# Hybrid DeltaNet / attention step: weight ring with a running place, dense stages written out straight, four output chunks side by side behind each norm, down projection begun on early rounded activations

## The reference, cut to what matters

```
layer 0: h = modulate(rmsnorm(x));  [gated DeltaNet || differential attention](h @ w_in) @ w_out
         h = modulate(rmsnorm(x));  x += gate * ((silu(h @ w_g) * (h @ w_u)) @ w_down)      # D_FF = 2816
layer 1: h = modulate(rmsnorm(x));  multi-head latent attention (w_in, w_uq, w_ukv, w_out)
         h = modulate(rmsnorm(x));  top-2-of-8 expert SwiGLU (D_FF = 1408 each)
modulate(x) = rmsnorm(x) * (1 + scale) + shift;  scale, shift, gate = silu(c) @ mod_w + mod_b
```

## Time and profile before

| | |
|---|---|
| median of 3 runs | 2804.85 us (2801.8 to 2806.8) |
| the profiled execution's own time | 2803.48 us |
| its span, first to last instruction | 2801.4 us |
| mean granted TensorE clock, share of full | 0.934 |
| TensorE busy | 2474.6 us (88%) |
| VectorE, ScalarE, GpSimd busy | 1040.2, 859.9, 442.3 us |

### The profile page before, as it was taken

One profiled execution on the slowest core, in us unless ns is written; L12 is line 12 of the kernel. 1 busy time (PEld: TensorE's weight loads), 2 busy tenths in 40 slices (PEclk: granted clock), 3 DMA queues, 4 the chain that ended last, 5 costly groups with the idle time before them and its releaser, 6 DMA issues.

```text
span 2801.4 us, 36871 instructions
## 1 busy us (share of the span) xinstructions
PE 2474.6 (88%) x14830; PEld 2089.0 (75%) x14831; DVE 1040.2 (37%) x1561; ACT 859.9 (31%) x1155; POOL 442.3 (16%) x196
## 2 busy tenths in 40 slices
PE   6999986888877899898998899987999888899894
PEld 3766665777775699898996546667988788798894
DVE  1211264444464221223211234313434677744544
ACT  2211233111100411212112213212434666644544
POOL 0000001233300200002000000004222444433411
PEclk9998997999998899999999999996999999999996
DMA  6002023533300220311120010003565788865754
GB/s 270 16 31 90 8 83 136 210 132 131 130 8 17 88 76 16 121 46 56 69 89 23 29 45 1 1 31 142 196 212 198 297 323 317 315 227 214 267 181 165
DMA packets 63207, 350.69 MB, mean 125 GB/s; under 512 B 6032, under 2 KB 11408, under 8 KB 30448
## 3 DMA queue, kind: packets, MB, share of 16 engines
q1 hardware_dynamic: 59440, 335.97, 32.5%
q0 software_dynamic: 3648, 12.95, 1.2%
HBM read 316.75 MB, written 32.15 MB: 125 GB/s over the span
## 4 chain that ended last, share of the span: by engine, by line
PE 45%; issue 13%; POOL 6%; DVE 4%; ACT 3%; DMA 1%; POOLq 0%; DVEq 0%; ACTq 0%; SPq 0%
PE ps L498 43%; POOL wring_x L1632 5%; PE ps L621 1%; PE ps L838 1%; DVE tmp L1174 1%; ACT hT L612 1%; POOL rows L1815 0%; DMA wring<-in_w_ukv 0%; ACT tmp L890 0%; PE ps L1726 0%; PE ps L1674 0%; DVE att L860 0%; ACT tmp_x L609 0%; DMA arena<-rows,att 0%; DVE tmp L1182 0%
## 5 line engine op out<-in xcount | busy, mean ns | idle before, releaser
L498 PE MATMUL ps<-hT,wring 128*128 128x320 f32 x1472 | 409.4, 441 | 22.1 <-ACT hT L612 10.4
L498 PEld LDWEIGHTS ps<-hT,wring 128*128 128x128 f32 x1472 | 285.1, 194 | 146.6 <-issue 21.0
L1632 POOL TENSOR_TENSOR wring_x<-wring,arena_x 128x2048 fp32r<-128x2048 f32 (+1 forms) x60 | 276.2, 4612 | 479.9 <-ACT arena_x L1626 479.9
L498 PE MATMUL ps<-arena_x,hT_x 128*128 128x256 f32 x2464 | 324.3, 288 | 12.3 <-issue 12.3
L498 PEld LDWEIGHTS ps<-arena_x,hT_x 128*128 128x128 f32 x2464 | 306.6, 194 | 15.9 <-issue 13.7
L1626 ACT ACTIVATE arena_x<-wring 128x2048 fp32r<-128x2048 f32 x153 | 283.2, 1854 | 91.2 <-DMA wring<-in_w_mgu 90.8
L498 PE MATMUL ps<-arena_x 128*128 128x512 f32 (+2 forms) x1144 | 251.2, 374 | 22.4 <-DVE arena_x L1801 13.3
L1632 DVE TENSOR_TENSOR wring_x<-wring,arena_x 128x2048 fp32r<-128x2048 f32 (+1 forms) x90 | 223.2, 2479 | 77.2 <-ACT arena_x L1626 77.2
L498 PEld LDWEIGHTS ps<-arena_x 128*128 128x128 f32 x1144 | 203.4, 202 | 52.2 <-issue 23.6
L498 PE MATMUL ps<-arena 128*128 128x128 f32 (+3 forms) x680 | 174.1, 411 | 7.0 <-ACT arena L890 4.8
L498 PE MATMUL ps<-tmp_x,arena_x 128*128 128x320 f32 x832 | 139.4, 320 | 30.2 <-ACT hT L612 12.4
(11 more groups left out here) (274 smaller groups left out, 2937.9 us busy)
## 6 DMA issues: line engine op xcount, KB each, us to landing
wring<-in_w_mgu SPq DMA_DIRECT2D x105, 1024.0 KB, 6.3
wring<-in_w_mod SPq DMA_DIRECT2D x48, 1024.0 KB, 4.8
wring<-in_w_mdn SPq DMA_DIRECT2D x30, 1024.0 KB, 5.0
wring<-in_w_gu SPq DMA_DIRECT2D x22, 1024.0 KB, 4.9
wring<-in_w_mdn SPq DMA_DIRECT2D x20, 768.0 KB, 4.4
wring<-in_w_ev SPq DMA_DIRECT2D x14, 1024.0 KB, 7.9
rows<-hT SPq DMA_DIRECT2D x1, 12288.0 KB, 33.4
wring<-in_w_dn SPq DMA_DIRECT2D x16, 704.0 KB, 5.2
```

The source lines that it names most:

```text
L498: return nc.tensor.matmul(out, lhsT, rhs, start=first, stop=last)
L1632: eng.tensor_tensor(wslot_x[s][:, 0:size], wslot[s][:, 0:size], whi[b % 6][:, 0:size].bitcast(F32), ALU.subtract).then_inc(ready, 1)
```

## The change

- A block's slot is its place in the order of all loads before the experts, modulo 5. A load waits for the block five places earlier. The zeroing DMA of 12 MB stays behind the fifth block of mod2.
- `pe_first`: behind norms 0 and 2 the first four output chunks are made side by side, tile by tile of h, in the four PSUM slots. In the dense SwiGLU the first four chunks (two gate, two up) are made so as well, the product with the remainder of h following two tiles behind; their third products come after.
- The stages mod, eo, fgu, fdn and oo lose their hardware loops on TensorE, VectorE and ScalarE and are written out; fgu is one turn of 22 blocks, so its PSUM slots run on.
- Down: tiles 16 to 19 of `actT` are rounded by ScalarE during gate/up (`act_early_lead`). The second half column of the first down weight is rounded before the first. Chunk 0 takes tiles 16 to 19 first, in the first two products, then each other tile in both as it comes, then the third product for all. GpSimd still makes the remainders of tiles 14 to 21, in that order.

```diff
-            s = j % wslots(stage)
-            return s, turn * per[s] + before[s] + j // wslots(stage)
+            if stage != "moe":
+                i = place[stage, j, turn]
+                return i % WS, i // WS
...
+                held = order[place[stage, j, turn] - WS] if n else None
...
+        def pe_first(stage, chunks_, h_base):
+            weights, slots = [cols(block(stage, c // 2), KD, 256, c % 2) for c in range(chunks_)], []
+            for k in range(KD):
+                nc.tensor.wait_ge(h_ready, h_base + k + 1)
+                for c in range(chunks_):
+                    if k == 0:
+                        slots.append(take(stage, c))
+                    for half in range(2):
+                        last = mm(pair(slots[c])[:, half, :], weights[c][k], from_h(k, half * HT, half * HT + HT),
+                                  k == 0, k == KD - 1)
+                    if k == KD - 1:
+                        last.then_inc(ps_full[slots[c]], 1)
...
         def pe_even_in():
-            for c in range(12):
+            pe_first("qkv", 4, 0)
+            for c in range(4, 12):
...
         def pe_ffn():
-            with nc.Fori(0, 2, engines=(mybir.EngineType.PE,), hint_back_edge=True) as turn:
...
+            nc.tensor.wait_ge(fhi_ready, 2)
+            for k in range(KD + 2):
+                for n, kk, ready in ((0, k, (h_ready, 8 + k + 1)), (1, k - 2, (hlo_ready, k - 1))):
+                    if not 0 <= kk < KD:
+                        continue
+                    nc.tensor.wait_ge(*ready)
+                    for c in range(4):
+                        if k == 0:
+                            slots.append(take("fgu", c))
+                        pe_gu(slots[c], fhi[:, c // 2, :], c % 2, n, kk)
+            nc.tensor.wait_ge(flo_ready, 2)
+            for c in range(4):
+                for k in range(KD):
+                    last = pe_gu(slots[c], wring_x[:, wuse("fgu", c // 2)[0], :], c % 2, 2, k)
+                last.then_inc(ps_full[slots[c]], 1)
...
+                    if first:
+                        steps = [(n, k) for k in LEADS[:4] for n in (0,)] + [(1, k) for k in LEADS[:4]]
+                        steps += [(n, k) for k in LEADS[4:] for n in (0, 1)] + [(2, k) for k in range(FC)]
+                    else:
+                        steps = [(n, k) for n in range(3) for k in range(FC)]
...
         LEFT = 14
+        LEADS = list(range(16, 20)) + list(range(16)) + [20, 21]
...
+        def act_early_lead(act, k):
+            done(act, "fgu", 2 * k + 1)
+            nc.scalar.activation(act_lead[k], actT[:, k, :], ACT.Copy).then_inc(lead_ready, 1)
...
         def act_lead_parts(act):
-            full(act, "fgu", 2 * EC - 1, 1)
-            for b in range(2):
+            full(act, "fgu", 2 * FC - 1)
+            for b in (1, 0):
                 act_dhi(act, b, 0)
-            for k in range(FC):
+            for k in LEADS[4:]:
                 nc.scalar.activation(act_lead[k], actT[:, k, :], ACT.Copy).then_inc(lead_ready, 1)
...
         def pe_odd_in():
-            for c in range(6):
+            pe_first("oi", 4, 16)
+            w = block("oi", 2)
+            for c in range(4, 6):
...
+            for j in range(FC):
+                if j + 2 < FC:
+                    act_fhi(act, j + 2)
+                act_gate(act, j)
+                if j - 1 in LEADS[:4]:
+                    act_early_lead(act, j - 1)
```

More of the change, by code:

```diff
@@ L371, in program @@
         }
[L372 to L382, removed]
-        def wuse(stage, j, turn=0):
-            before, per, _, _ = W.stages[stage]
-            s = j % wslots(stage)
-            return s, turn * per[s] + before[s] + j // wslots(stage)
+        order = [(stage, j, turn) for stage, (_, _, each, turns, _) in loads.items() if stage != "moe"
+                 for turn in range(turns) for j in range(each)]
+        place = {what: i for i, what in enumerate(order)}
+        def wuse(stage, j, turn=0):
+            if stage != "moe":
+                i = place[stage, j, turn]
+                return i % WS, i // WS
+            s = j % (WS + 1)
+            before = (len(order) - s + WS - 1) // WS if s < WS else 0
+            per = (EC + 6 - s + WS) // (WS + 1)
+            return s, turn * per + before + j // (WS + 1)
         def block(stage, j, turn=0):
@@ L415, in load_stage @@
             each, turns = loads[stage][2:4]
[L416 to L430, removed]
+            for turn in range(turns):
+                for j in range(each):
+                    load(sync, stage, j, turn)
+                    if (stage, j) == ("mod2", WS - 1):
+                        sync.wait_ge(s_zero, 1)
+                        sync.dma_start(rows_dram[IT:(ITEMS + 1) * IT, :].rearrange("(m p) c -> p m c", p=P),
+                                       spread(Sst[0], 1, 2 * ITEMS)).then_inc(y_rows_out, 16)
         def items_of(eng):
@@ L554, in pe_mod @@
             nc.tensor.wait_ge(crow_ready, 1)
-            with nc.tensor.Fori(0, MOD_FIRST // 2) as i:
+            for i in range(MOD_FIRST // 2):
                 for j in range(2):
@@ L580, in dve_mod @@
             dve_crow(dve, st)
-            with dve.Fori(0, MOD_FIRST // 2) as i:
+            for i in range(MOD_FIRST // 2):
                 for j in range(2):
@@ L1248, in dve_residual @@
         def dve_residual(dve, stage, each, turns, gate):
-            with dve.Fori(0, turns) as turn:
+            for turn in range(turns):
                 for j in range(each):
@@ L1262, in dve_residual_chunk @@
             last.then_inc(ps_free[s], 1)
-        def pe_ffn():
[L1268 to L1286, removed]
```

142 lines of the change are left out of this document (75 added, 67 removed).

## The result

The changed kernel takes 2768.9 us (median of 4 runs, 2768.1 to 2773.8), the one before 2804.3 on the same chip: ratio 0.988, interval [0.9865, 0.9896]. The gain is 35.4 us where 57 was forecast, and the time lies just above the range. The profiled execution took 2768.8 us, its span 2766.8.

A forecast was written before the change was run, and what follows sets the result against it. TensorE, busy in 88% of the span, was taken as the bound, with time won only where it stands or runs slowly. Terms summed to 57.2 us, from 2803.5 to 2746.3, stated as a 2747 us median; range 2731 to 2768.

The forecast's parts named there:

- start: Mod stage: with five blocks in flight x lands by 36.5 us, so norm 0's squares begin earlier; gain 7.5 us.
- z, qk, chunks behind norm 0: Layer 0: weights loaded stages ahead gain 6.7 us at z, 4.9 at qk; four chunks side by side gain 0.5.
- behind norm 1, edge of the turns: Gate and up: filling without gaps and full clock early gain 10.7 us; no stand or slow start between turns gains 11.6.
- down: Down's first chunk: weights lie ready, but GpSimd's remainders hold its end and chunk 1 starts slow; gain 2.6 us.
- chunks behind norm 2, kn, vv: Side-by-side chunks gain 0.5 us; waits and slow starts that go gain 5.0 at kn and 7.2 at vv.
- some 5 us either way: Experts' loops: allowance in the range because their code moves; the sum itself gave them no gain or loss.
- Rival C: Written-out SwiGLU: 17 late instruction packets at 4.9 us each add 83 us, making the kernel slower, 2830 us; chance 0.03.
- Rival A: Only loads pay: clock stays low in the filling, down gives nothing, x comes no sooner; 2763 us; chance 0.12.
- B: Rival: remainders do not hold down back, x and norm 1 reach their upper ends; 2736 us; chance 0.05.
- D: Rival: in one stage a load still waits, leaving a stall of 5 to 12 us; 2752 to 2759 us; chance 0.10.

The follow-up runs named there:

- pad128: Changed kernel plus 32 one-column matmuls (128 instructions) in TensorE's idle time ahead of the router; 2750.5 us, ratio 0.9806.
- pad192: Changed kernel plus 192 instructions of one-column matmuls, 32 matmuls ahead of the router and 16 ahead of the first gather; 2782.2 us, ratio 0.9919.
- pad384: Changed kernel plus 384 instructions, 80 one-column matmuls ahead of the router and 16 ahead of the first gather; total not compared, experts' part 836.5 us.
- no_first: Changed kernel without the side-by-side chunks behind norms 0, 1 and 2; 2791.3 us, ratio 0.9971.
- old_down: Changed kernel with the old order of down's first chunk: no early rounding, three products one after the other; 2775.8 us, ratio 0.9909.
- place_only: Changed kernel with only the written-out loops and running slots kept, side-by-side chunks and early down undone; 2794.8 us, ratio 0.9969.
- straight_only: Changed kernel with only the written-out loops kept; running slots, side-by-side chunks and early down undone; 2830.3 us, ratio 1.0095.

## Why the prediction was wrong, point by point

| term | forecast | measured |
|---|---|---|
| start | 7.5 | 6.7 |
| z, qk, chunks behind norm 0 | 12.1 | 11.3 |
| behind norm 1, edge of the turns | 22.3 | 21.7 |
| down | 2.6 | 3.4 |
| chunks behind norm 2, kn, vv | 12.7 | 10.8 |
| latent attention and up to the experts | 0 | -5.7 |
| experts | 0, "some 5 us either way" | -13.6 |

(From the table of stages; gate and up took 333.9 us before and 312.2 after, down up to norm 2 171.8 and 168.4. Two slips of the working change nothing: 2746.3 and 1.4 are 2747.7, and 17 packets over the 504 us from 958 to 1462 are one in 30 us, not 27.)

**The step that failed** is the last of the range: "some 5 us either way for the experts' loops, whose code moves", in a sum that gave them nothing. Their place is worth 32 us between pad128 and pad192, and the change moved them from a good place (27 packets, 846.9 us) to a worse one (46 packets, 860.5 us). Of the 22.6 us by which the sum of 57.2 exceeds the 34.6 of the profiled spans, 13.6 are this, 5.7 lie between the start of the latent attention and the experts, to which the sum gave nothing either, and 3.3 in the other terms. What mattered was in the trace and the code: stands of "issue" in front of items' first matmuls, a loop with branches, a longer stream ahead of it. I looked for the cost of instruction supply only where the code changes.

**Rival C** had the mechanism and the wrong stage. The written-out SwiGLU shows no break: TensorE has no stand of "issue" from the first gate/up matmul to the end of gate and up, and one of 1.5 us ahead of down, where ScalarE rounds the first half column. Straight code is free here, as said: the packets of this stretch up to norm 2 are 25 where the kernel before has 20. The prediction counted 17 packets for it as new, because two loops held most of that code before; but those loops had their 20 too. Of the 26 packets more, 19 are in the experts' part, which the prediction did not count. **The rule of the Trainium skill** ("Runtime: NRT & Kernel Launch", Instruction fetch mechanics), that a taken branch whose target isn't in the fetched window waits for a fetch, I set aside because eo's loop edge shows no stand. The experts' loop agrees with it: in the changed kernel packets start within 0.5 us of the beginning and of the end of the stands of 5.41 and 5.80 us at the second and third item, the latter where groups of 16 instead of 32 matmuls show the other branch. That section's pages of 256 instructions agree with pad384; its statement that crossing into the next page is mostly hidden agrees with the straight part.

**Clock.** 4.4 us of the loss lie in the latent attention. Windows at its start, in the changed kernel and in the one before:
```profile
1596.00:1600.00 4.00, 4.00 (x8) 1.61 (x7) 1.37 (x3) 1.05 (x3) 0.00 (x0) 0.50 0.00 0
1600.00:1604.00 4.00, 4.00 (x9) 1.90 (x9) 0.96 (x2) 0.00 (x0) 0.00 (x0) 0.50 0.00 0
```
```profile
1650.00:1654.00 4.00, 4.00 (x17) 1.87 (x16) 2.05 (x4) 1.05 (x3) 0.00 (x0) 1.00 0.48 203
```
With the same matmuls behind the same 1.3 us of idle time the clock is at 1.2 GHz in both windows of one and at 2.4 GHz in the other. Another 1.8 us are the same thing behind norm 2 (16.7 us from the squares to oi instead of 14.9). Removing a part doesn't show a cause: no_first and old_down have the attention at 158.1 us, place_only has 167.7. But it isn't chance between executions either: the eight profiles of kernels with all parts of the change (the changed one, its four paddings and the three versions with early remainders) all have 162.9 us. The stretch behind norm 2 does vary: pad128 and pad384 are the same kernel up to norm 3, and it is slow in one profile (16.8) and not in the other (15.0). That costs nothing by itself, since from the first gate/up matmul to the attention both take 652.9 us. What sets the clock in the attention stays open.

**What held.** The side-by-side chunks: TensorE in the filling with one gap of 0.49 us, clock back four microseconds in, 10.7 forecast, 10.1 measured up to chunk 4, and 11.6 and 13.0 when taken out. Down: GpSimd as what is late next, chunk 1 at 30.2 forecast and 30.5 measured. The pace had an error that cancelled: the last pairs come 1.5 us apart, not two, and GpSimd's first two remainders took 7.07 us, not 5.41. The forecast left open how little of the 2.6 us was the early order's, and old_down says none. The qk stage kept its slow start. The start, the edge, kn and vv came within 2 us of their terms (the edge 9.7 between place_only and straight_only, for 11.6). Rival A (loads alone pay) is refuted by the filling and by x at 37.3 us, B by chunk 0, D by the waits. With the experts' loop at a good place, as in pad128, the kernel is at 2750.5 us, ratio 0.9806, where 2747 was forecast; the loop is then 3.5 us faster than in the kernel before.

## What to carry to other kernels

A program with a loop of branches at its end can feel instructions added ahead of it: before a change to straight code is judged, its loops should be tried at a few places (one-column matmuls in idle time will do), or the gain may be read as 35 us when it is 54. A ring of buffers should run on over stages and turns instead of starting again at slot 0. To start a stage early, move the work of the engine that ends it: rounding four tiles early gave nothing until GpSimd had only two remainders left at the end.

## What the runs showed of the hardware

- 128 instructions of nothing on TensorE's queue ahead of a branched hardware loop took 18 us off one kernel and put 20 us on another; 64, 128 and 192 gave 863.6, 843.4 and 875.8 us for the same loop (one profile each).
- The instruction queue's packets in that loop tell a good place from a bad one: 26 or 27 with 837 to 851 us, 46 with 861 to 876 us.
- In the changed kernel the stands of 5.41 and 5.80 us at an item's edge began and ended within 0.5 us of the start of a packet of that queue (2008.4 and 2014.1 us, 2118.4 and 2124.0). In straight code the same queue moved 25 packets from the first gate/up matmul to norm 2 with one stand of 1.5 us; as two hardware loops, that stretch had 20.
- A shift of 384 instructions had the packets and the stands of one of 128.
- GpSimd's remainders of 128x640 tiles let TensorE go on every 1.5 us while VectorE was idle for most of the time; one took 3.5 us (7.07 for two) and 4.5 us (8.95 for two) beside VectorE's remainders.
- The same matmuls of the latent attention, behind the same 1.3 us of idle time, began at 2.4 GHz in some kernels (158.1 to 158.5 us) and fell to 1.2 GHz in others (162.9 us in eight profiles, 167.7 in one).
